# Raw prenorms, gates inside the latent attention, head pairs, diagonal norms and the recurrence inside its projection

## The reference, cut to what matters

```python
# block 1
f = swiglu(rmsnorm(h, ffn1_pre_g), ...);      h = h + 0.5 * rmsnorm(f, ffn1_post_g)
m = hybrid_mixer(rmsnorm(h, mix_pre_g), ...); h = h + rmsnorm(m, mix_post_g)
f = swiglu(rmsnorm(h, ffn2_pre_g), ...);      h = h + 0.5 * rmsnorm(f, ffn2_post_g)
# hybrid_mixer: one projection, two attentions (8 heads each), two gates
y_sb  = stick_breaking_attention(sb_q, sb_k, sb_v) @ w_sb_o
y_mla = latent_attention(q_nope, q_rope, k_nope, k_rope, v, cid) @ w_mla_o
g = sigmoid(gate_pre + b_gate)                # 2 x 1024 columns of the projection
out = (g_sb * y_sb + g_mla * y_mla) @ w_out
# stick breaking, per head, scale and strict mask
log_1m = where(strict, log_sigmoid(-z), 0.0); csum = cumsum(log_1m)
a = where(strict, exp(log_sigmoid(z) + csum[-1] - csum), 0.0)
# block 2, twice: mixer, conv_ffn, gate * (p @ w)
#   mixer 0: RG-LRU recurrence and mLSTM from one projection of 3080 columns
#   mixer 1: banded attention, 16 heads, 4 key heads, window 128, with sinks
```

## Time and profile before

| what | value |
|---|---|
| median of 3 runs | 2963.38 us (2956.52 to 2976.5) |
| the profiled execution | 2966.62 us |
| its span | 2964.9 us |
| TensorE busy | 2761.7 us (93%) |
| VectorE, ScalarE, GpSimd busy | 1201.9, 909.8, 1077.5 us |
| mean granted TensorE clock | 0.936 |
| chain that ended last | TensorE 86%, VectorE 8%, ScalarE 2% |

### The profile page before, as it was taken

One profiled execution on the slowest core, in us unless ns is written; L12 is line 12 of the kernel. 1 busy time (PEld: TensorE's weight loads), 2 busy tenths in 40 slices (PEclk: granted clock), 3 DMA queues, 4 the chain that ended last, 5 costly groups with the idle time before them and its releaser, 6 DMA issues.

```text
span 2964.9 us, 34880 instructions
## 1 busy us (share of the span) xinstructions
PE 2761.7 (93%) x13196; PEld 2181.3 (74%) x13196; DVE 1201.9 (41%) x1416; ACT 909.8 (31%) x1343; POOL 1077.5 (36%) x539
## 2 busy tenths in 40 slices
PE   6999989999989988999979869999998869999999
PEld 5999978973356766888848538888877637888887
DVE  3112131103452473122257265667225674666412
ACT  3222223235422213222233523222224364222223
POOL 4343444421210144444435224444443202444443
PEclk9999999998775789999989979999999989999999
DMA  3222321210110121222313002332322201323322
GB/s 138 92 88 74 89 89 65 93 45 0 38 36 1 36 78 58 98 98 79 101 52 100 29 29 94 98 96 95 105 94 79 71 1 57 99 92 99 107 93 71
DMA packets 65649, 219.16 MB, mean 74 GB/s; under 512 B 8401, under 2 KB 8529, under 8 KB 65554
## 3 DMA queue, kind: packets, MB, share of 16 engines
q1 hardware_dynamic: 63792, 216.42, 22.6%
q10 hardware_dynamic: 1762, 1.45, 0.2%
HBM read 215.74 MB, written 2.10 MB: 73 GB/s over the span
## 4 chain that ended last, share of the span: by engine, by line
PE 86%; DVE 8%; ACT 2%; issue 2%; POOL 1%; DMA 0%; SPq 0%; ACTq 0%; PEldq 0%; DVEq 0%; PEld 0%; POOLq 0%
PE PS L289 25%; PE PS L290 25%; PE PS L291 25%; PE PS L1468 1%; PE PS L1491 1%; PE PS L1085 1%; PE PS L1114 1%; PE PS L1101 1%; DVE ntmp L487 1%; PE PS L1099 1%; PE PS L2322 1%; PE PS L1478 1%; PE PS L1493 1%; DVE h L606 1%; DVE ast__141 L2368 1%
## 5 line engine op out<-in xcount | busy, mean ns | idle before, releaser
L284 POOL TENSOR_TENSOR wlo<-wraw,whi 128x1024 fp32r<-128x1024 f32 (+3 forms) x425 | 988.2, 2326 | 1582.7 <-ACT whi L277 1582.7
L289 PE MATMUL PS<-xh,whi 128*128 128x512 f32 (+2 forms) x2544 | 902.5, 355 | 30.9 <-DVE xl L458 21.7
L290 PE MATMUL PS<-xl,whi 128*128 128x512 f32 (+2 forms) x2544 | 897.6, 353 | 0.0
L291 PE MATMUL PS<-xh,wlo 128*128 128x512 f32 (+2 forms) x2544 | 897.1, 353 | 0.0
L277 ACT ACTIVATE whi<-wraw 128x1024 fp32r<-128x1024 f32 (+3 forms) x425 | 429.0, 1010 | 1024.0 <-PE PS L291 1020.3
L289 PEld LDWEIGHTS PS<-xh,whi 128*128 128x128 f32 (+1 forms) x2544 | 478.2, 188 | 112.3 <-issue 23.8
L291 PEld LDWEIGHTS PS<-xh,wlo 128*128 128x128 f32 (+1 forms) x2544 | 479.4, 188 | 66.4 <-issue 1.4
L290 PEld LDWEIGHTS PS<-xl,whi 128*128 128x128 f32 (+1 forms) x2544 | 479.1, 188 | 63.9 <-issue 0.5
L289 PE MATMUL PS<-hid2h,whi 128*128 128x512 f32 x560 | 217.8, 389 | 0.0
L290 PE MATMUL PS<-hid2l,whi 128*128 128x512 f32 x560 | 217.8, 389 | 0.0
L291 PE MATMUL PS<-hid2h,wlo 128*128 128x512 f32 x560 | 217.8, 389 | 0.0
(11 more groups left out here) (406 smaller groups left out, 3456.9 us busy)
## 6 DMA issues: line engine op xcount, KB each, us to landing
wraw<-w_up_dram SPq DMA_DIRECT2D x96, 512.0 KB, 3.3
wraw<-w_dn_dram SPq DMA_DIRECT2D x48, 512.0 KB, 3.3
wraw<-w_f1gu_dram SPq DMA_DIRECT2D x44, 512.0 KB, 3.3
wraw<-w_f2gu_dram SPq DMA_DIRECT2D x44, 512.0 KB, 3.3
wraw<-w_win_dram SPq DMA_DIRECT2D x34, 512.0 KB, 3.2
wraw<-w_hyin_dram SPq DMA_DIRECT2D x24, 512.0 KB, 3.3
wraw<-w_pg_dram SPq DMA_DIRECT2D x16, 512.0 KB, 3.3
wraw<-w_f1dn_dram SPq DMA_DIRECT2D x16, 384.0 KB, 3.2
```

Source lines behind the costliest of these rows:

```text
L284: pool.tensor_tensor(wlo[:, s, 0:size], wraw[:, s, 0:size], whi[:, s, 0:size].bitcast(F32), ALU.subtract).then_inc(lo_done.s, 1)
L289: pe.matmul(out_, whi[:, s, a:b], xhi, start=start, stop=False, skip_group_check=True)
L290: pe.matmul(out_, whi[:, s, a:b], xlo, start=False, stop=False, skip_group_check=True)
L291: return pe.matmul(out_, wlo[:, s, a:b], xhi, start=False, stop=stop, skip_group_check=True)
```

## The change

Nothing of the mathematics changes but the order of products.

- **Raw prenorms everywhere.** `s_prenorm` and `rsq` go. `s_load` scales tiles by the gain alone; `s_post_raw` replaces `s_postnorm` + `s_prenorm`: VectorE does all scale, add and low steps, ScalarE high parts and squares; the sum of squares of f is taken during s_out from PSUM. Gate/up multiplies the factor `rbx` in at both evacuations. After a boundary the first four chunks (three and the gate columns in hyin) take each input tile in turn (`OUTER`). Barriers there go. vec loads before con, x tiles 2 to 7 behind the first weight chunk.
- **Gates in the latent attention.** win is 18 chunks; `gate` is a stream of 16 in `s_latent`, four input tiles (twelve matmuls) per unit; Sigmoid moves to `s_mix`. `s_mla_project` makes scaled x again for it. p·v uses one PSUM bank, the gates the other.
- **Head pairs in stick.** 20 units over (pair, j); maxima split into high and low fp32r parts on VectorE; the sums are fp32r matmuls; the mask is added by a matmul; no GpSimd work.
- **Recurrence inside hyin.** `s_hyif`, `s_hyin`, `s_rglru` become one stage; the gate products come after chunks 5 and 6, the rest is spread over later chunks. In `s_mlstm` GpSimd cuts the weights before the product. `s_hyout` takes three tiles ahead of the last head.
- **Diagonal norms in the banded attention.** The band is added by a matmul, Exp reads PSUM with the scale, and 1/sum goes into a diagonal matrix by which turn multiplies.
- `s_ple_gate` follows a tile one step later; `s_qkv` takes its first two chunks tile by tile.

```diff
-("win", 34, SLOT), ("hyif", 1, 64)
+("win", 18, SLOT), ("gate", 16, SLOT), ("hyif", 1, 288)
...
 # s_load
+                load_x(sp, (0, 1))
+                sp.dma_start(vec[:, :], d["vec"]).then_inc(vec_landed.s, 16)
...
 # s_post_raw, DVE
+                dve.wait_ge(*rbc_done(1))
+                scale(0)
+                add(0)
+                for t in range(DT):
+                    if t + 1 < DT:
+                        scale(t + 1)
+                    scaled_low(dve, t)
+                    if t + 1 < DT:
+                        add(t + 1)
+                    if t >= 1:
+                        added(dve, t - 1)
...
 # s_latent, PE
+                def gate(n):
+                    c, kt = divmod(n, DT)
...
+                    if kt == 0:
+                        pe.wait_ge(*lo_done(g + 1))
+                        if c:
+                            pe.wait_ge(*gate_out(c))
...
+                    ins = mm3(pe, PS3[:, 7, :], s, kt * P, (kt + 1) * P, xh512[:, kt, :], xl512[:, kt, :],
+                              kt == 0, kt == DT - 1)
...
                     if u + 2 < NU:
                         scores(u + 2)
+                    gate(4 * u)
+                    gate(4 * u + 1)
                     turn(u)
+                    gate(4 * u + 2)
                     if u >= 1:
                         pv(u - 1)
+                    gate(4 * u + 3)
...
 # s_latent, DVE
+                def gate(c):
+                    dve.wait_ge(*chunk_used(gate_base + c + 1))
+                    dve.tensor_tensor(gates[:, c, :], PS3[:, 7, :], rbx[:, 0:T], ALU.mult).then_inc(gate_out.s, 1)
...
+                    if u % 2 == 0 and u >= 2:
+                        gate(u // 2 - 1)
...
 # s_stick
-            units = [(hd, j) for hd in range(HEADS) for j in (3, 2, 1, 0, 4)]
+            units = [(p, j) for p in range(4) for j in (3, 2, 1, 0, 4)]
...
+                        for x in range(3, j if j < 4 else -1, -1):
+                            for tile in (sph, spl):
+                                pe.matmul(PS3[0:m, 2 * (u % 3) + hd, P * x:T], negr[:, 0:m], block(tile, p, x)[:, hd, :],
+                                          start=False, stop=False, skip_group_check=True)
...
+                    dve.tensor_copy(part(u, False), full).then_inc(hi_done_.s, 1)
+                    dve.wait_ge(*hi_done_(u + 1))
+                    dve.tensor_tensor(part(u, True), full, part(u, False).bitcast(F32), ALU.subtract).then_inc(lo_done_.s, 1)
...
 # s_hyin, PE
+                    if c in (5, 6):
+                        pe_lru_gates(pe, 2 * c - 10)
...
+                if t0 == 0:
+                    pe.wait_ge(*taps(16))
+                    pe.wait_ge(*rw_in(64))
...
 # s_hyin, DVE
+                for c in range(24):
+                    scale(c)
+                    if 1 <= c < 5:
+                        conv_rg(c - 1)
+                    if c == 3:
+                        dve_scan(dve)
...
 # s_mlstm
-                    pool.wait_ge(*st_done(u + 1))
-                    b = mst[:, u % 4, P * j:P * (j + 1)]
+                    pool.wait_ge(*w_done(u + 1))
+                    b = msw[:, u % 4, P * j:P * (j + 1)]
...
 # s_window
+                    for a in range(2):
+                        ins = pe.matmul(sc_ps(u, k0(u))[:, 2 * a:2 * a + 2, :], identr[:, :], band2, start=False, stop=True,
...
-                            ins = pe.transpose(PS[:, 2048 + (2 * x + b) * P:2048 + (2 * x + b + 1) * P],
-                                            asx[:, u % 2, x, b * P:(b + 1) * P], c_("ident"))
+                            ins = pe.matmul(PS[:, 2048 + (2 * x + b) * P:2048 + (2 * x + b + 1) * P],
+                                            asx[:, u % 2, x, b * P:(b + 1) * P], diag[:, u % 2, x, :], start=True,
...
-                    dve.scalar_tensor_tensor(a, sc_ps(u, k0(u)), 0.125, band4, ALU.mult, ALU.add).then_inc(sc.s, 1)
...
-                    dve.tensor_tensor(a, a, m4, ALU.mult).then_inc(pn.s, 1)
+                    dve.tensor_tensor(diag[:, u % 2, :, :], eye4, m4, ALU.mult).then_inc(diag_done.s, 1)
```

More of the change, by code:

```diff
@@ new lines, in pe, with act @@
+                pe.wait_ge(*last_squared)
+                for i in range(H):
+                    ins = pe.matmul(PS3[:, 6 + i, 0:w], c_("ones"), sq[:, i * w:(i + 1) * w], start=False, stop=True,
+                                    skip_group_check=True)
+                ins.then_inc(total.s, 1)
+            def act(act):
+                act.wait_ge(*total(1))
+                act.activation(lnv[:, 0:n].rearrange("p (a q) -> p a q", a=H), bank(6, H, w), ACT.Ln,
+                               bias=epsc[:, 0:1], scale=1.0 / D).then_inc(ln_done.s, 1)
+                act.wait_ge(*ln_done(1))
+                act.activation(rbc[:, 0:n], lnv[:, 0:n], ACT.Exp, bias=epsc[:, 2:3] if factor == 0.5 else 0.0,
+                               scale=-0.5).then_inc(rbc_done.s, 1)
+                for t in range(DT):
+                    scaled_high(act, t)
+                    squared(act, t)
@@ new lines, in pe @@
+                if H == 2:
+                    for k in range(4):
+                        if k == 3:
+                            pe.wait_ge(*con_landed(16))
+                            pe_root(pe)
+                            pe.wait_ge(*rb_done(1))
+                        chunk(0, k, k == 0)
+                    with pe.Fori(1, turns) as j:
+                        turn(j)
+                    return
+                for kt in range(OUTER):
+                    xn_ready(pe, xn, kt)
+                    for k in range(4):
+                        s, _, g = slot_of(base, k, 4, 0)
+                        if kt == 0:
+                            pe.wait_ge(*lo_done(g + 1))
+                        tile(pe, k, s, kt, 4)
@@ L1027, in dve @@
                 n = 0
-                for t in range(5):
-                    dve.wait_ge(*tile_read["win"](12 + t + 1))
+                for c in range(count):
+                    take(c)
+                    if 10 <= c < 14:
+                        keep(c - 10)
+                    if not 12 <= c < 17:
+                        continue
+                    t = c - 12
+                    dve.wait_ge(*read(c + 1))
                     total = acc if t < 3 else sq
@@ L1088, in sums @@
+                    if j < 4:
+                        for hd in range(2):
+                            ins = pe.matmul(PS3[:, 2 * (u % 3) + hd, c0:c0 + P], identr, maskr, start=False, stop=False,
+                                            skip_group_check=True)
+                    ins.then_inc(z_done.s, 1)
                 def sums(u):
-                    hd, j = units[u]
+                    p, j = units[u]
                     m = rows(u)
                     pe.wait_ge(*sp_done(u + 1))
-                    pe.wait_ge(*sp_cut(cut(u)))
@@ new lines, in sums @@
+                    ins.then_inc(arg_done.s, 1)
+                def pv(u):
+                    p, j = units[u]
+                    c0, m = first(j), rows(u)
+                    pe.wait_ge(*a_done(u + 1))
+                    if p >= 2 and j == 3:
+                        pe.wait_ge(*y_lo(p - 1))
+                        pe.wait_ge(*y_hi(p - 1))
+                    for hd in range(2):
+                        r = 64 * hd
+                        ins = pe.matmul(PS3[r:r + 64, 6 + p % 2, c0:T], vs[0:m, j, (2 * p + hd) * 64:(2 * p + hd + 1) * 64],
+                                        aa[0:m, u % 2, hd, c0:T], start=(j == 3), stop=(j == 4), skip_group_check=True)
+                    ins.then_inc(pv_done.s, 1)
@@ L1848, in dve_high, with spx, pox, s_rglru_out @@
+            spa, poa = weights("hyif")
+            spb_, pob = weights("hyin")
+            def spx(e):
+                spa(e)
+                spb_(e)
+            def pox(e):
+                poa(e)
+                pob(e)
+            stage(pe, act, dve, pox, spx)
+            return scaled, v_kept, read, gated, key_scaled
+        def s_rglru_out(gated):
+            high, low = local("lru", high=1, low=1)
             def dve_high(dve):
-                Chain(dve, "dve_chain").link(dve.tensor_copy(yh[:, 0:4, :], grg[:, :, :]))
+                dve.wait_ge(*gated(1))
+                dve.tensor_copy(yh[:, 0:4, :], grg[:, :, :]).then_inc(high.s, 1)
```

1458 lines of the change are left out of this document (814 added, 644 removed).

## The result

The changed kernel takes 2751.9 us (median of 4 runs, 2751.02 to 2752.45) against 2959.95 for the kernel before; the ratio is 0.934, with a 95% interval of 0.925 to 0.942. The forecast was 2755. One of the four runs of the kernel before took 2921.94 us and the other three 2956.52 to 2976.5; against that one alone the ratio is 0.942. The sum was right to 3 us, but three of its terms were not; the experiments say why.

What follows compares the result with a forecast made beforehand. TensorE was taken to bound the kernel, busy 2761.7 of 2964.9 us. The terms summed to -208.7 from the profiled 2966.6, so 2758, less 3 for the runs' median: 2755 us, range 2695 to 2830.

Steps and rivals of the forecast that it cites:

- Start: Kernel start: gate/up stream needs only weights and tile 0, root factor multiplied in at evacuation; -21 us, bounds -15 and -23.
- Boundaries: After f1dn and wout: TensorE's wait for the next stage's tiles shrinks from 34.7 us lost to 10; -24.5 and -24.
- Gates out of win: Input projection win: sixteen of 34 chunks leave, 384 matmuls at 0.2285 us each; -87.7 us.
- Latent: Latent attention: gate matmuls among the units lift TensorE's clock, stage 160 us instead of 136; +24.
- The rival at 301 us: Latent stage stays at the lower clock level with the gates added: 301 us, kernel 2896; chance .05.
- Stick: Stick attention: head pairs, fp32r sums and no GpSimd cuts shorten 138 us to 113; -25.
- The bound of 100: Stick attention: shortest length expected, 100 us, from 75 us of engine work plus a third for latency.
- Recurrence and mlstm: Boundary n4 through recurrence -14.5, mlstm with cut and recurrence's VectorE steps out of its chain -15, early hyout -6.
- Taps: Input projection hyin: new TensorE wait of 13 us for VectorE's convolution taps, bounds 0 and 25.
- Banded attention: Banded attention: VectorE's pass over scores goes, TensorE then sets units at 5.0 instead of 5.74 us; -9, bounds -20 and +6.
- ple_gate and qkv: ple_gate into qkv: TensorE's 6.7 us of standing and a last tile's wait of 2.3 go; -9, bounds -2 and -12.
- the streams: Gate/up streams: two more VectorE multiplications per turn, hidden by the stream itself; 0.

Runs made afterwards that it cites:

- the first experiment: Changed kernel with the 16 gate chunks as one block ahead of the latent attention instead of between its units: 2747.4 us against 2751.9.
- the primed run: Kernel before with eight extra fp32 products, results unused, right ahead of its latent attention: 2913.1 us against 2965.7.
- the combined one: Changed kernel with gates as a block, transposes for turn in the banded attention and the mlstm gate scan behind the fourth convolution: 2737.6 us against 2751.9.

## Why the prediction was right, and where it was not

- **Start (-21; -18.0).** The first product was put at 11.4 and came at 11.25. Two things were put at nothing: the first 21 matmuls stand 0.22 us apart where later ones stand 0.12, 2.1 us, though the granted clock in the rows is 1.00 there; and at 17.28 TensorE waits 1.1 us for a tile's low part. The wait for the root factor was 1.5 us, inside the 3 that the sum had for the root.
- **Boundaries (-24.5, -24; about -18.4 and -21.6).** The chain to the first tile is right to half a microsecond. The step that failed is what follows: tiles come every 3.26 us, so eight need 26 us, and four chunks hold 22 us of work; I had put 1 us there. At n2 there is another step that the sum did not have: of the 6.1 us missing, 5.0 are the three waits at the transposes of v.
- **Gates out of win (-87.7).** With 18.4 for the boundary the window's 106.1 agrees; the block of the same 384 matmuls took 89.9 in the first experiment.
- **Latent (+24; +38.9).** The total has two mis-sized terms. The attention's own work at the upper level is not 66 but 76 us (TensorE busy from 870 to 949 in the primed run, whose stage takes 79.6), and the stage still starts low (0.88 in its first 28 us), which costs 3.4 (6.9 us at half the clock). These are 13.4 of the 17.8 us by which the stage passed 160; the rest stays open. The mechanism, that plain matmuls lift the clock, is true, but what I took from it is not: that they had to stand among the units. Of the Trainium skill ("TensorE: Matmul & The Clock Gate", Part 4) the prediction used the rule that transposes do not count as activity; the stage with its transposes held 1.00 through 79 us without any gate, so here they did not pull it down. The rival at 301 us did not come about: the gates' matmuls ran at the upper level inside the stage and as a block.
- **Stick (-25; -46.8).** The bound of 100 was too high: the stage took 95.9. (The -25 is also two thirds of the way from 138 to 100 and not six tenths, which would be -23.) The split passes on VectorE, 57 us in the sum, cost 7.7 us at most, and the clock rose to 0.93. The fp32r form is 17.7 of the gain.
- **Recurrence and mlstm (-14.5 - 15 - 6; -30.0).** Nearly right in sum, wrong in part. From f2dn's end to the mlstm's first product it is 179.1 us where it was 190.5: 11.4 gained, 14.5 forecast. The shorter wait for the taps helped; against it stand the wait of 5.2 for the root factor, for which the sum had 1 at the boundary and a stall of 2, and the 6.0 at the transposes of v, for which it had nothing. From there to the end of hyout it is 113.8 where it was 132.3: 18.5 gained, 21 forecast. Of that the early start of hyout carries 8.2 and VectorE's steps gone from the chain 5.8; the cut, named first in the -15, is worth nothing that can be told; 4.5 stay open.
- **Taps (a wait of 13; 5.3).** Same place, same cause, too long. The three taps after the first take 2.33 us (0.78 each) where no GpSimd instruction runs, against the mean of 1.425 that I used; beside one (1397.74 to 1400.19) they take 4.29. That makes 3.8 us less in four convolutions; the gate scan took 5.2 us (1390.12 to 1395.36) instead of 8.4:

```profile
1378.11 2.33 DVE L1779 SCALAR_TENSOR_TENSOR xc<-xrg,vec,xc 128x512 f32<-128x512 f32 x3
...
1396.45 4.29 DVE L1779 SCALAR_TENSOR_TENSOR xc<-xrg,vec,xc 128x512 f32<-128x512 f32 x3
...
1397.74 2.45 POOL L289 TENSOR_TENSOR wlo<-wraw,whi 128x1024 fp32r<-128x1024 f32 x1 [8.09 <-ACT whi L282]
```

- **Banded attention (-9; -21.1).** That TensorE bounds the unit was right. The diagonal product takes 0.235 us (1.88 for eight), not 0.33, so that a steady unit is 4.53 and not 5.0. The first full units come 3.2 to 4.1 us apart, so the mean step between the twelve is 4.25 where it was 5.72: 16.2 us. From the last unit's scores to the end of the stage, which the sum left out, it is 12.3 us where it was 16.8. That VectorE's gain was the larger part was not seen: the experiment without the diagonal is faster still.
- **ple_gate and qkv (-9; -10.1)** and the streams (0; 0) came as forecast.

The misses, in the order of the stages, are +3 (start), +6.1 (n2 and win), -21.8 (stick), -0.5 (mla_project), +14.9 (latent), -1.8 (mix, wout), +2.4 (n3), +5.5 (n4 to hyout), -1.1 (ple, qkv) and -12.1 (banded attention): 69 us of misses whose sum is -5.5. The total was right partly by luck.

## What to carry to other kernels

A stage of short products on TensorE can sit at half the clock only because of what ran just ahead of it: put a few products ahead of it and look at the granted clock before rebuilding the stage. Here that gave 52.6 us for two lines of code. When a sum of many terms fits, measure the terms one by one all the same: here one of them (the diagonal) was a loss of 10 us under a gain of 31. When a factor moves from the input to the evacuation, look for what then stands behind the evacuation on its engine: the copies of the turned v come late here, and TensorE waits 10 us in all for them. When the next stage needs late tiles, let several chunks share each tile, and count tiles by their spacing, not by the first one.

## What the runs showed of the hardware that was not expected

- The same instruction sequence held either level of TensorE's clock for over 75 us: 0.50 in 138.9 us with TensorE busy 99% of the time, 1.00 in 79.6 us with 96%. What came ahead of it decided. In two runs (the first experiment and the combined one) the level fell and rose again inside the stage. What made it rise there stays open.
- Eight fp32 products of 96x512 (7.1 us) between two waits of 0.7 us, which stayed, were worth 52.6 us.
- A VectorE instruction that reads one SBUF tensor was also long beside GpSimd's split: the softmax multiply of 528 columns took 1.85 us at 751.35 while GpSimd ran a split from 750.51 to 752.90. All eight multiplies of that size met a split and took 1.84 to 1.85 us; in the kernel before, where no split runs in this stage, the eight took 0.50.

```profile
750.12 0.43 DVE L1655 TENSOR_SCALAR pm<-pm,st 128x400 f32<-128x400 f32 x1
...
750.51 2.39 POOL L289 TENSOR_TENSOR wlo<-wraw,whi 128x1024 fp32r<-128x1024 f32 x1 [8.42 <-ACT whi L282]
...
751.35 1.85 DVE L1655 TENSOR_SCALAR pm<-pm,st 128x528 f32<-128x528 f32 x1
```

What it cost the stage was not measured; gate matmuls stood behind it on TensorE. The Trainium skill ("SBUF — State Buffer", Who interferes with whom) says so of such instructions in their two-port mode; these rows agree.
